# Meta-token columns dropped behind the attention, and the last norm made with tokens on the rows

## What is computed

```python
mix = jnp.concatenate([y_ssd, y_sb], axis=-1) @ w_out[l]        # 2048 -> 1024
h = h + rms_norm_2(mix, mix_post_g[l])
xn = rms_norm_2(h, ffn_pre_g[l])
gu = xn @ w_up[l]                                               # 1024 -> 2 x 2816
g = causal_dwconv(gu[..., :D_FF], ffn_conv_w[l], ffn_conv_b[l]) # 3 taps along the tokens
f = (jax.nn.gelu(g, approximate=True) * gu[..., D_FF:]) @ w_down[l]
h = h + rms_norm_2(f, ffn_post_g[l])
return h[:, N_META:]                                            # the 512 real tokens
```

## Time and profile before

| | us |
|---|---|
| median of 3 runs | 1788.29 (1787.34 to 1788.85) |
| profiled execution | 1791.05 |
| its span, first to last instruction | 1788.9 |
| TensorE busy | 1640.7 (92%) |
| GpSimd busy | 915.8 (51%) |
| DVE busy | 1016.1 (57%) |
| ACT busy | 487.2 (27%) |

### The profile page before, as it was taken

How to read it: one execution, slowest core, us unless ns; L and a number is a source line. 1 busy time by engine, 2 the same in 40 slices (tenths; PEclk the granted TensorE clock), 3 DMA queues, 4 the chain that set the end, 5 groups by cost and what they waited for, 6 DMA issues and landing times.

```text
span 1788.9 us, 31233 instructions
## 1 busy us (share of the span) xinstructions
PE 1640.7 (92%) x11688; PEld 1452.7 (81%) x11688; DVE 1016.1 (57%) x1524; ACT 487.2 (27%) x979; POOL 915.8 (51%) x838
## 2 busy tenths in 40 slices
PE   5799998977999999897898999999996999999996
PEld 3687865865888888797887877887896999999995
DVE  3777315237545885785776887776336555553003
ACT  3211012012025663222223555554212111110001
POOL 0454420343575343475535764444473677777771
PEclk9899999987999999898999999999996999999997
DMA  7354410113320001222111111111131223323331
GB/s 271 116 202 152 146 59 0 36 35 103 97 82 13 2 25 36 59 83 70 36 35 48 48 48 48 47 48 48 48 95 48 70 83 93 94 83 89 94 90 56
DMA packets 208385, 131.37 MB, mean 73 GB/s; under 512 B 5246, under 2 KB 194206, under 8 KB 208174
## 3 DMA queue, kind: packets, MB, share of 16 engines
q1 hardware_dynamic: 208302, 130.21, 24.0%
HBM read 128.10 MB, written 2.10 MB: 73 GB/s over the span
## 4 chain that ended last, share of the span: by engine, by line
PE 79%; DVE 14%; ACT 3%; issue 2%; DMA 1%; SPq 0%; DVEq 0%; POOL 0%; ACTq 0%; POOLq 0%
PE ps L1960 20%; PE ps L1961 19%; PE ps L1963 19%; PE ps L2217 2%; PE ps L2243 2%; PE ps L2511 2%; DVE sb_sum L1802 1%; PE ps L2139 1%; PE ps L2421 1%; PE ps L2204 1%; DVE seg L1722 1%; PE ps L2195 1%; PE ps L2486 1%; DVE op_lo L1283 1%; DVE sq L1240 1%
## 5 line engine op out<-in xcount | busy, mean ns | idle before, releaser
L680 POOL TENSOR_SCALAR w_hi<-raw 128x512 fp32r<-128x512 f32 x370 | 308.4, 834 | 752.3 <-PE ps L1963 390.5
L682 POOL TENSOR_TENSOR w_lo<-raw,w_hi 128x512 fp32r<-128x512 f32 x370 | 514.7, 1391 | 30.9
L1960 PE MATMUL ps<-op_hi,w_hi 128*128 128x512 f32 x704 | 256.6, 365 | 23.5 <-DVE op_lo L1283 15.2
L1960 PE MATMUL ps<-xn_hi,w_hi 128*128 128x264 f32 x848 | 247.6, 312 | 11.9 <-ACT zs L1046 3.1
L1961 PE MATMUL ps<-op_lo,w_hi 128*128 128x512 f32 x704 | 243.2, 361 | 0.0
L1961 PE MATMUL ps<-xn_lo,w_hi 128*128 128x264 f32 x848 | 225.8, 287 | 0.0
L1963 PE MATMUL ps<-op_hi,w_lo 128*128 128x512 f32 x704 | 211.5, 360 | 0.0
L1960 PE MATMUL ps<-u_hi,w_hi 128*128 128x264 f32 x704 | 189.7, 289 | 8.5 <-DVE u_lo L1861 6.6
L1961 PE MATMUL ps<-u_lo,w_hi 128*128 128x264 f32 x704 | 188.7, 289 | 0.0
L1960 PEld LDWEIGHTS ps<-op_hi,w_hi 128*128 128x128 f32 x704 | 135.3, 192 | 65.5 <-DVE op_lo L1283 12.7
L1960 PEld LDWEIGHTS ps<-xn_hi,w_hi 128*128 128x128 f32 x848 | 161.4, 190 | 27.1 <-issue 15.2
(11 more groups left out here) (369 smaller groups left out, 3086.6 us busy)
## 6 DMA issues: line engine op xcount, KB each, us to landing
raw<-in_w_in SPq DMA_DIRECT2D x45, 512.0 KB, 3.8
raw<-in_w_up SPq DMA_DIRECT2D x44, 512.0 KB, 3.8
ada_ring<-in_ada_w SPq DMA_DIRECT2D x16, 1024.0 KB, 6.2
raw<-in_w_in_ab SPq DMA_DIRECT2D x20, 512.0 KB, 3.9
raw<-in_w_in_c SPq DMA_DIRECT2D x20, 512.0 KB, 3.8
ada_first<-in_ada_w SPq DMA_DIRECT2D x4, 2048.0 KB, 19.9
raw<-in_w_out SPq DMA_DIRECT2D x16, 512.0 KB, 4.1
raw<-in_w_down SPq DMA_DIRECT2D x16, 512.0 KB, 4.1
```

The costliest lines, as they stand in the source:

```text
L680: steps(nc.gpsimd.tensor_scalar(hi, r, 1.0, 0.0, ALU.mult, ALU.add))
L682: nc.gpsimd.tensor_tensor(lo, r, hi.bitcast(F32), ALU.subtract)\
L1960: mm(o[:, 512 * b:512 * b + n], w_h[:, k, :], hi[:, k0 + k, c0:c0 + n], start=a, stop=False)
```

## The change

A constant `CUT` = 12 drops the first twelve of the sixteen meta columns behind the attention; four are kept. `T3` = 516 columns remain, as two segments of 258 (`SEG_3`).

- The output product, the norm of mix, `xT`, `u_hi`, `u_lo` and the gate slabs work on 516 columns; the value slabs of `up` on the 512 real tokens, as one segment (`SEG_LAT`); the convolution writes only the 512.
- `f_hi`, `f_lo` and `down` have 512 columns as one segment (`SEG_F`): 3 matmuls a chunk instead of 6.
- The sums for the norm of `xT` no longer go through DVE. ACT squares each chunk right behind its `u_hi`, and TensorE sums each chunk's square by itself (`ffn_sums`: ten matmul instructions of one column), inside the first up slab, behind that chunk's products.
- At the same place TensorE transposes each chunk of `xT` (four transposes, `turn_x_tok`), and ACT copies them into `x_tok`, tokens on the partitions. This was done at the very end before.
- Behind each block of down ACT copies it to one of two `fT` buffers; TensorE transposes it (four transposes, `turn_f`) behind the first slab of the next block; ACT squares it there with a running sum (four operations of 128 columns), and DVE multiplies it by the gain, which now lies along the row and is loaded once for all partitions (`g_bc`).
- Behind the last block: copy, transposes, squares, a reduction of the sums, root, reciprocal, and then for each of four tiles of tokens one DVE operation of 1024 columns, `x_tok + fg * rstd`, whose result is stored. The sums over partitions, the spread rows, `add_normed("fin")`, the final transposes and `y_out` are gone.

```diff
@@ constants and segments
+CUT = META - 4
+T3 = T2 - CUT
+HALF3 = T3 // 2
+        SEG_3 = [(CUT, HALF3), (CUT + HALF3, HALF3)]
+        SEG_LAT = [(META, S)]
+        SEG_F = [(0, S)]
@@ SP, between the loads for up and for down
+            sp.dma_start(g_bc[:, :], ffn_post_g_2.partition_broadcast(P)).then_inc(s["g_in"], 16)
@@ ACT, behind the norm of mix
+            def take_x_tok(k):
+                act.wait_ge(s["x_tok_turned"], k + 1)
+                nc.scalar.copy(x_tok[:, :, k * P:(k + 1) * P], tok4(x_tok_ps(k))).then_inc(s["x_tok_taken"], 1)
             for k in range(KC):
                 act.wait_ge(s["norm_done"], 8 + k + 1)
-                nc.scalar.activation(u_hi[:, k, :], xT[:, k, :], ACT.Identity, scale=col("ffn_pre", k))\
+                nc.scalar.activation(u_hi[:, k, CUT:T2], xT[:, k, CUT:T2], ACT.Identity, scale=col("ffn_pre", k))\
                   .then_inc(s["op_hi"], 1)
-            norm_squares("ffn")
+                act.wait_ge(s["sq_used"], 8 * k0 + max(k - 1, 0))
+                nc.scalar.activation(sq3[:, k % 2, CUT:T2], xT[:, k, CUT:T2], ACT.Square).then_inc(s["sq"], 1)
+                if k:
+                    take_x_tok(k - 1)
+            take_x_tok(KC - 1)
+            norm_std("ffn")
@@ ACT, down
+            def f_squares(b):
+                act.wait_ge(s["ft_turned"], b + 1)
+                for t in range(S // P):
+                    ins = nc.scalar.activation(f_sq[:, t, :], ft_ps(b)[:, t * P:(t + 1) * P], ACT.Square,
+                                               accum_out=stat_f[:, t, b:b + 1])
+                ins.then_inc(s["ft_sq"], 1)
+            for b in range(KC):
+                if b:
+                    f_squares(b - 1)
+                act.wait_ge(s["slab_done"], block_done("down", b + 1))
+                nc.scalar.copy(fT[:, b % 2, :], gemm_ps[(b0 + b) % 2][:, 0:S]).then_inc(s_evac[(b0 + b) % 2], 1)
+            f_squares(KC - 1)
@@ DVE
             add_normed("post", ffn_lo)
-            norm_adds("ffn")
             norm_rstd("ffn")
-            dve.wait_ge(s["op_ready"], OP_DONE["ffn"] + FC)
-            stream_adds("fin")
-            add_normed("fin")
+            def f_gain(b):
+                dve.wait_ge(s["ft_sq"], b + 1)
+                nc.vector.tensor_tensor(fg[:, :, b * P:(b + 1) * P], tok4(ft_ps(b)),
+                                        g_bc[:, b * P:(b + 1) * P].unsqueeze(1).to_broadcast([P, S // P, P]), ALU.mult)\
+                  .then_inc(s["ft_used"], 1)
+            for b in range(KC - 1):
+                f_gain(b)
+            dve.wait_ge(s["ft_sq"], KC)
+            nc.vector.tensor_reduce(stat[:, 0:4], stat_f[:, :, :], AX.X, ALU.add).then_inc(s["fin_sum"], 1)
+            f_gain(KC - 1)
+            dve.wait_ge(s["fin_std"], 1)
+            steps(nc.vector.reciprocal(rstd[:, 0:4], stat[:, 4:8]))
+            for t in range(S // P):
+                nc.vector.scalar_tensor_tensor(x_tok[:, t, :], fg[:, t, :], rstd[:, t:t + 1], x_tok[:, t, :],
+                                               ALU.mult, ALU.add).then_inc(s["out_ready"], 1)
@@ TensorE
-            gemm("up", u_hi, u_lo, SEG_2, ready=OP_DONE["sbn"], beside=lambda: sums_end("ffn"))
-            gemm("down", f_hi, f_lo, SEG_2, ready=OP_DONE["ffn"], cuts=DOWN)
-            sums_end("fin")
+            def turn_x_tok(k):
+                if k >= 2:
+                    pe.wait_ge(s["x_tok_taken"], k - 1)
+                for t in range(S // P):
+                    ins = nc.tensor.transpose(x_tok_ps(k)[:, t * P:(t + 1) * P],
+                                              xT[:, k, META + t * P:META + (t + 1) * P], ident[:, :])
+                ins.then_inc(s["x_tok_turned"], 1)
+            def ffn_sums(k):
+                ...
+                pe.wait_ge(s["sq"], 8 * k0 + k + 1)
+                for t, (c0, n) in enumerate(tiles):
+                    ins = mm(o[0:n, t:t + 1], sq[:, k % 2, c0:c0 + n], ones[:, 0:1], start=False, stop=True,
+                             skip_group_check=True)
+                ins.then_inc(s["sq_used"], 1)
+                ...
+            gemm("up", u_hi, u_lo, SEG_3, ready=OP_DONE["sbn"], beside=lambda: sums_rows("ffn"), odd_segs=SEG_LAT,
+                 each=beside_up)          # beside_up(k): turn_x_tok(k), then ffn_sums(k); first slab only
+            def turn_f(i, jb):
+                ...
+                for t in range(S // P):
+                    ins = nc.tensor.transpose(ft_ps(1 - jb)[:, t * P:(t + 1) * P], fT[:, 1 - jb, t * P:(t + 1) * P],
+                                              ident[:, :])
+                ins.then_inc(s["ft_turned"], 1)
+            gemm("down", f_hi, f_lo, SEG_F, ready=OP_DONE["ffn"], cuts=DOWN, between=turn_f)
+            turn_f(KC // 2, 0)
```

More of the change, by code:

```diff
@@ L499, in sb_steps, with x_tok_ps, ft_ps @@
             return SBN + (SB_SKEW if last else 0)
+        def x_tok_ps(k):
+            return bank(7) if k % 2 == 0 else gemm_ps[(BLOCK0["up"] + 1) % 2][:, 512:1024]
+        def ft_ps(b):
+            return bank(4 + b % 2)
         block = stack.enter_context(nc.Block())
@@ L1168, in take_mix @@
             def take_mix(k, src):
-                nc.scalar.copy(two(mixT[:, k, :]), halves(src)).then_inc(s["mix_a"], 1)
+                nc.scalar.copy(two(mixT[:, k, CUT:T2]), seg3(src)).then_inc(s["mix_a"], 1)
             def take_early(k):
@@ L1216, in _ @@
                 nc.scalar.copy(f_hi[:, bass.ds(i, 1), :], fgl[:, :].unsqueeze(1)).then_inc(s["ffn_hi"], 1)
[L1217 to L1221, removed]
+            nc.scalar.preload_act_table_set("sqrt_and_others")
+            b0 = BLOCK0["down"]
+            def f_squares(b):
[10 more added lines that the diff above has]
+            f_squares(KC - 1)
+            act.wait_ge(s["fin_sum"], 1)
+            nc.scalar.activation(stat[:, 4:8], stat[:, 0:4], ACT.Sqrt, bias=eps[:, 0:1], scale=1.0 / D)\
+              .then_inc(s["fin_std"], 1)
         @block.vector
@@ L1235, in add_squares @@
                 dve.wait_ge(s["sq"], 8 * k0 + 1 + k)
-                n = sum(n for _, n in tiles)
+                c0 = tiles[0][0]
+                c1 = c0 + sum(n for _, n in tiles)
                 if k0 or k:
                     dve.wait_ge(s["sq_used"], 8 * k0 + k)
-                nc.vector.tensor_tensor(sq[:, 2, 0:n], sq[:, 2, 0:n], sq[:, slot, 0:n], ALU.add)\
+                nc.vector.tensor_tensor(sq[:, 2, c0:c1], sq[:, 2, c0:c1], sq[:, slot, c0:c1], ALU.add)\
                   .then_inc(s["sq_used"], 1)
@@ L1947, in sums_rows, with products @@
                 ins.then_inc(s["rstd_rows"], 1)
-            def products(o, hi, lo, w_h, w_l, kn, k0, segs, first, last, slab_end=True, ready=None, rest=None):
+            def products(o, hi, lo, w_h, w_l, kn, k0, segs, first, last, slab_end=True, ready=None, rest=None, each=None):
                 for k in range(kn):
@@ L1964, in products, with gemm @@
                                  stop=z)
-                if slab_end:
+                    if each is not None:
+                        if z and slab_end:
+                            ins.then_inc(s["slab_done"], 1)
+                        each(k0 + k)
+                if slab_end and each is None:
                     ins.then_inc(s["slab_done"], 1)
-            def gemm(name, hi, lo, segs, ready=None, cuts=((0, KC),), beside=None):
+            def gemm(name, hi, lo, segs, ready=None, cuts=((0, KC),), beside=None, odd_segs=None, each=None, between=None):
                 per, g0, b0 = PER[name], SLAB0[name], BLOCK0[name]
@@ L1984, in body @@
                             pe.wait_ge(s["split_half"], g0 + j + 1 + u * per * i)
-                            products(gemm_ps[b % 2], hi, lo, w_hi[:, slot, :, :], w_lo[:, slot, :, :], kn, k0, segs,
+                            products(gemm_ps[b % 2], hi, lo, w_hi[:, slot, :, :], w_lo[:, slot, :, :], kn, k0,
+                                     odd_segs if odd_segs and jb else segs,
                                      h == 0, h == per - 1, ready=ready if jb == 0 else None,
-                                     rest=g0 + j + 1 + u * per * i)
+                                     rest=g0 + j + 1 + u * per * i,
+                                     each=each if ready and jb == 0 else None)
+                            if between and h == 0:
+                                between(i, jb)
                 body(0, ready)
@@ new lines, in ffn_sums @@
+            def ffn_sums(k):
+                k0, tiles, _, sq, _ = NORMS["ffn"]
+                o = pair_ps[1]
+                if k == 0:
+                    mm(o[:, 0:NT], zeros[:, :], zeros[:, 0:NT], start=True, stop=True)
+                pe.wait_ge(s["sq"], 8 * k0 + k + 1)
[3 more added lines that the diff above has]
+                ins.then_inc(s["sq_used"], 1)
+                if k == KC - 1:
+                    pe.wait_ge(s["sq_used"], 8 * k0 + KC)
+                    pe.sem_inc(s["ssq"], 1)
```

102 lines of the change are left out of this document (55 added, 47 removed).

## The result

The changed kernel takes 1779.67 us (median of six runs, 1776.84 to 1781.01), the kernel before 1787.82 (six runs, 1785.79 to 1788.85): a ratio of 0.9944, with a 95% interval of 0.9929 to 0.9959. Forecast were 1776.8, a range of 1762.0 to 1781.5, and faster. The profiled execution took 1780.02, its span 1778.2; that of before 1791.05 and 1788.9.

A forecast was written before the change was run, and what follows sets the result against it. TensorE was taken as the bound, busy 92% of the span. Gains 1.5 + 7.8 + 2.3 + 13.9 less 14.0 gave 11.5 us: 1779.5 for the profiled execution, 1776.8 as median; 8-in-10 range 1762 to 1781.5.

The forecast's parts named there:

- The start of up: First up slabs until dense work at full clock: added sums and transposes make TensorE the bound, a loss of 14.0 us.
- first rival: First up slab: the clock rises within it, 0.6 us gained instead of 14.0 lost, total 1762.2 us; chance 0.19.
- a first slab above 30 us: Sign that the forecast is right: first up slab of 30 us or more, no gap, granted clock 0.50.
- The second slab: Second up slab: 24 matmuls of 512 columns, 11 at half clock (4.7 us), then 13 at full (3.0 us).
- two stretches: Evidence for half clock: an earlier operand's wait, 403 to 417, and single-column sums from 1273.15 on.
- The stretch with the sums: Kernel before, 1273 to 1277: single-column sums busy without a gap while the clock fell, mean 0.74 over 1275 to 1280.
- The end: Last product matmul to the kernel's end: 27.7 us becomes 13.8, a gain of 13.9, bounds 13 to 15.5.
- the squares: Behind the last down block: four ACT squares of 128 columns, each with an accumulator read, 1.8 us.
- Output product: Eleven dense output slabs at 258 columns: 0.13 us less each, 1.5 us gained.
- the two bounds: Price of a 258-column matmul: the 264 price (no gain) or by columns, 0.1188 us; the second was taken.
- Up and down: Dense up pairs gain 7.8 us over 21 pairs; down blocks gain a net 2.3 us after added transposes.
- the load of the gains: New load on SP's queue between up's and down's loads: costed at nothing, 4 us once if cover fails.

The follow-up runs named there:

- the first experiment: The changed kernel measured once more without any edit, as the base for the other runs: 1780.06 us, ratio 0.9949 to the kernel before.

## Why the prediction was right, and where it wasn't

**The start of up** decided, as the prediction had it, and the choice between the forecast and its first rival fell on the right side: a first slab above 30 us, no gap, a clock of 0.50, the rise in the second slab. Of its terms: 4.27 us a chunk came where 4.1 were put (1.43 for the products, restart included, where 1.29 stood; 0.99 for the transposes instead of 0.8; 1.85 for the sums instead of 2.0), 34.8 against 33.3. The second slab took 8.16 where 7.7 stood. What was missing altogether is a second fall, from 1400.2 to 1403.6 (the row of 1400 to 1404 above): I let the clock stay up once it had risen, though rows' matmuls and a wait of 1.88 us lie between. What brings that fall stays open: with the short fillers the same rows and the same wait of 1.88 us were followed by a clock of 1.00 (1387 to 1402). Together 17.3 against 14.0; this is the largest error.

The Trainium skill (TensorE: Matmul & The Clock Gate, section on why this matters for your kernels) has the engine at full clock when it is kept busy continuously. The prediction went against that on the strength of two stretches, one of them with single-column sums, and six kernels with such sums bear its choice out (the changed one, the one without `CUT`, the two that move a part to the second slab, and the two with fillers): busy 34.53 of 35 us at 0.50, and busy 14.00 of 14 at 1.00 with the clock falling right behind. In this kernel what TensorE does counts, not only whether it is busy.

The stretch with the sums was read too strongly, though. The prediction says that the clock fell during the sums of 1273 to 1277. The sums, from 1273.15 to 1276.4, ran wholly at the full clock; it fell at 1277.4, among products without a gap, and was back at 1280.9. Two stretches of the kernel before:

```profile
1273.00:1276.60 3.60, 3.60 (x34) 3.48 (x34) 0.00 (x0) 0.60 (x1) 3.15 (x4) 1.00 0.00 0
1276.60:1280.00 3.40, 3.40 (x20) 3.40 (x20) 0.62 (x4) 0.21 (x1) 0.59 (x1) 0.62 0.45 133
```

That the sums brought this fall was thus only argued, from the order of events; what shows it for this kernel are the experiments.

**The end** gained 15.7 where 13.9 stood, just above the bounds given (13 to 15.5); the forecast's terms add up to 13.7 and not 13.8. The mis-sized term is the squares: four with their reads take 1.2 us (1767.91 to 1769.08), not 1.8, since the read of the accumulator overlaps the next square: they start 0.25 apart. The small parts around them (reduction, `fg`, reciprocal) took 0.9 against 1.4, and DVE's last operation to the end 3.35 against 3.7.

**Output product.** Forecast by columns, 0.1188 a matmul; measured 0.1202. ACT's squares of the results of two successive slabs, before and then changed:

```profile
1333.02 0.65 ACT L1201 ACTIVATE sq<-mixT 128x528 f32<-128x528 f32 x1 [5.21 <-DVE mixT L1868]
1338.87 0.65 ACT L1201 ACTIVATE sq<-mixT 128x528 f32<-128x528 f32 x1 [5.21 <-DVE mixT L1868]
```

```profile
1334.73 0.64 ACT L1222 ACTIVATE sq<-mixT 128x516 f32<-128x516 f32 x1 [5.13 <-DVE mixT L1920]
1340.50 0.63 ACT L1222 ACTIVATE sq<-mixT 128x516 f32<-128x516 f32 x1 [5.13 <-DVE mixT L1920]
```

A slab takes 5.77 instead of 5.85, so 0.08 and not 0.13 is gained, 0.9 over eleven; and the first one ends 0.5 later behind its last operand. That leaves 0.35 of 1.5. The price lies in the middle between the two bounds that the prediction named.

**Up and down.** Twenty pairs from one `gp` to the last one take 227.60 us (1407.29 to 1634.89), 11.38 each; before 233.95 (1393.22 to 1627.17), 11.70. The value slab is the forecast's 5.60, the gate slab 5.78 instead of 5.70, by the same price of 258 columns. Down came as worked out: seven blocks from 1655.79 to 1766.57, 15.83 each, which is 66 matmuls of 512 and 0.43 for the transposes; nothing of the load of the gains shows. GpSimd and DVE set no pace.

**What the sum hides.** A gain of 11.5 us was forecast; 8.2 came between the medians, and 10.7 between the two traces. The 10.7 are closer to the forecast than the parts are: -3.3 at the start of up, -1.2 and -1.0 in the products, -0.95 in front of up (the clock fell before the sums there, which took 1.99; 1.18 in the profiled execution of the first experiment), +1.8 at the end, and +3.9 ahead of the output product, of which 3.4 aren't the change's: that the traces come so near is luck. The range held the time, near its upper end.

## What to carry to other kernels

Before work is moved into a wait of TensorE, ask how it uses the array: at the half clock a chunk of products and transposes took 2.13 us (1355.01 to 1357.14, with the sums in the second slab), with ten single-column sums 4.27, and with two streamed sums 2.57 (1355.83 to 1358.40). The same sums thus cost 2.14 us one way and 0.44 the other. The first way also kept everything around it at half; the second let the clock rise and turned a gain of 0.5% into one of 2.0%. A "hidden" step needs its own sum against the wait that hides it: here the first slab grew to 34.8 us where its operands came in 10.4. And a slab time is taken from the results of two successive slabs in the trace, since a price by columns is a bound only.

## What the runs showed of the hardware that I had not expected

- A full clock falls when single-column sums are mixed in, though the engine has next to no idle time: after 14.7 us of the slab in one run, 9.8 in another, and 2.8 us after the first sums behind products and transposes (1371.4 to 1374.2). Products with transposes (0.50, then 1.00 from 1359.6 and 1360.5 on) let it rise.
- A float32 matmul of 128 columns is two instructions of 0.11 to 0.12 us each (44 in 5.16 us, 88 in 9.99); a transpose of the same size is one (four in 0.43).
- ACT's read of its accumulator overlaps the next square: 0.25 us for both, where the rows alone, 0.28 and 0.20, would add to 0.48.
- DVE's reciprocal over 516 columns takes 3.38 us, where its copy of as many takes 0.70; it pays only where it is hidden.
